# The first mixer takes x times the norm's weights, its tiles are multiplied by the root as they leave PSUM, and the opening is reordered

## The reference

```python
hn = rmsnorm(h, norm_mix_g)            # h * rsqrt(mean(h*h) + eps) * g, mean over the 2048 features
proj = hn @ w_in + b_in
(q, k, v, o_pre, i_pre, f_pre, cb, cc, ch, gm_pre, gc_pre) = jnp.split(proj, offs, axis=-1)
hm = mlstm_chunkwise(q, k, v, i_pre, f_pre)      # 4 heads, q and k 128 wide, v 256 wide
hm = hm * rsqrt(mean(hm*hm) + EPS) * mlstm_head_g * sigmoid(o_pre)
y_m = hm @ w_branch_m
y_c = (cb * causal_dwconv(cc * ch, conv_w)) @ w_branch_c
merged = sigmoid(gm_pre) * y_m + sigmoid(gc_pre) * y_c
h = h + merged @ w_out
```

## Time and profile before

| | us |
|---|---|
| median of 3 runs (lowest, highest) | 2176.17 (2174.1, 2178.84) |
| the profiled execution's own time | 2177.88 |
| its span, first to last instruction | 2175.8 |
| TensorE busy, matmuls | 2110.0 (97%) |
| VectorE busy | 1313.0 (60%) |
| ScalarE busy | 1159.3 (53%) |
| GpSimd busy | 280.0 (13%) |

### The profile page before, as it was taken

How to read it: one execution, slowest core, us unless ns; L and a number is a source line. 1 busy time by engine, 2 the same in 40 slices (tenths; PEclk the granted TensorE clock), 3 DMA queues, 4 the chain that set the end, 5 groups by cost and what they waited for, 6 DMA issues and landing times.

```text
span 2175.8 us, 46737 instructions
## 1 busy us (share of the span) xinstructions
PE 2110.0 (97%) x17596; PEld 2071.1 (95%) x17596; DVE 1313.0 (60%) x1662; ACT 1159.3 (53%) x1558; POOL 280.0 (13%) x325
## 2 busy tenths in 40 slices
PE   5999999999999999999999999999999979999996
PEld 5999999999999999999999999999998969999996
DVE  5656655444457777777775555575665565766644
ACT  5444545555445656565655444645555445566643
POOL 2000000000110111111111101111001123111112
PEclk8999999999999999999999999999999989999998
DMA  4455455555555555555555655455444533444443
GB/s 153 170 179 190 172 175 197 185 200 193 185 188 206 193 193 193 193 193 193 193 193 195 224 218 209 173 180 194 174 158 171 192 135 136 175 154 156 171 174 116
DMA packets 54927, 393.83 MB, mean 181 GB/s; under 512 B 6097, under 2 KB 6225, under 8 KB 7522
## 3 DMA queue, kind: packets, MB, share of 16 engines
q1 hardware_dynamic: 54432, 392.19, 50.4%
q10 hardware_dynamic: 450, 1.02, 0.1%
HBM read 391.09 MB, written 2.10 MB: 181 GB/s over the span
## 4 chain that ended last, share of the span: by engine, by line
PE 83%; issue 11%; DVE 2%; POOL 2%; ACT 1%; DMA 0%; DVEq 0%; POOLq 0%; ACTq 0%; SPq 0%
PE acc L574 24%; PE acc L575 24%; PE acc L576 24%; PE tok L619 2%; PE tok L621 2%; PE tok L620 2%; POOL sumsq_g L1983 1%; PE att L647 1%; POOL n_lo L1992 0%; PE att L878 0%; PE att L879 0%; POOL x L2005 0%; DVE w_lo L1385 0%; DVE rstd L1393 0%; PE att L821 0%
## 5 line engine op out<-in xcount | busy, mean ns | idle before, releaser
L1385 DVE TENSOR_TENSOR w_lo<-raw,w_hi 128x1024 fp32r<-128x1024 f32 x740 | 904.1, 1235 | 710.9 <-ACT w_hi L955 708.5
L955 ACT ACTIVATE w_hi<-raw 128x1024 fp32r<-128x1024 f32 x740 | 768.3, 1056 | 552.1 <-PE acc L576 295.1
L574 PE MATMUL acc<-n_hi,w_hi 128*128 128x256 f32 x3488 | 974.2, 279 | 23.9 <-POOL n_lo L1992 20.3
L575 PE MATMUL acc<-n_lo,w_hi 128*128 128x256 f32 x3488 | 968.7, 278 | 0.0
L576 PE MATMUL acc<-n_hi,w_lo 128*128 128x256 f32 x3488 | 968.6, 278 | 0.0
L574 PEld LDWEIGHTS acc<-n_hi,w_hi 128*128 128x128 f32 x3488 | 658.9, 189 | 27.3 <-issue 20.5
L575 PEld LDWEIGHTS acc<-n_lo,w_hi 128*128 128x128 f32 x3488 | 659.7, 189 | 0.5
L576 PEld LDWEIGHTS acc<-n_hi,w_lo 128*128 128x128 f32 x3488 | 658.9, 189 | 0.0
L574 PE MATMUL acc<-f_hi,w_hi 128*128 128x256 f32 x688 | 189.9, 276 | 0.0
L575 PE MATMUL acc<-f_lo,w_hi 128*128 128x256 f32 x688 | 189.9, 276 | 0.0
L576 PE MATMUL acc<-f_hi,w_lo 128*128 128x256 f32 x688 | 189.9, 276 | 0.0
(11 more groups left out here) (324 smaller groups left out, 2959.7 us busy)
## 6 DMA issues: line engine op xcount, KB each, us to landing
raw<-stream_in SPq DMA_DIRECT2D x370, 1024.0 KB, 4.8
x<-x_in SPq DMA_DIRECT2D x4, 512.0 KB, 7.6
out<-x SPq DMA_DIRECT2D x4, 512.0 KB, 2.7
v_bias<-v_bias_in ACTq DMA_DIRECT2D x1, 512.0 KB, 8.9
par<-params_in ACTq DMA_DIRECT2D x1, 287.0 KB, 5.5
pos_i<-positions_in ACTq DMA_DIRECT2D x1, 128.0 KB, 6.8
gk<-gk_in ACTq DMA_DIRECT2D x1, 68.0 KB
```

The lines of the kernel that those rows point to most:

```text
L574: nc.tensor.matmul(out, w_hi[:, s, wc], hi[:, k, :], start=first, stop=False)
L575: nc.tensor.matmul(out, w_hi[:, s, wc], lo[:, k, :], start=False, stop=False)
L955: nc.scalar.activation(w_hi[:, s, :], raw[:, s, :], ACT.Copy).then_inc(hi_ready, 1)
L1385: nc.vector.tensor_tensor(w_lo[:, s, :], raw[:, s, :], w_hi[:, s, :].bitcast(fp32), ALU.subtract).then_inc(lo_ready, 1)
```

## The change

The first layer's matmuls take x * g, without the root. ScalarE makes `n_hi` from x and the weights (`first_high`) and VectorE `n_lo` (`first_low`), tile by tile as x arrives; GpSimd's part and the normed tiles go. The squares come later: ScalarE makes them after the first six units (`first_squares`), VectorE adds them to one tile (`squares_step`), and TensorE adds that over partitions with two fp32r matmuls in the middle of head 0's values.

Loads: SP loads x group 0, the gates' first unit, x group 1, the queries' first unit, x groups 2 and 3, and then the second units of both. Positions and value bias move from ScalarE's queue to SP's, behind units 4 and 5. TensorE does the gates' first half, the queries' first half, and then both second halves side by side, tile by tile. The gates go to `att[0]` instead of an accumulator.

Every tile of the heads and of the merge's gates is taken from PSUM by VectorE with a multiplication by `rstd` (`scaled_out`). ScalarE's bias and sigmoid steps then work in place in SBUF, after the split of the same j instead of before it. Values (tokens on partitions) are multiplied by a column `rcol` that TensorE makes from `rstd` with two small matmuls.

Head 0 is written out ahead of the loop, which runs over heads 1 to 3. In it the order is: queries, keys, values (with the sum of squares after two units), output gates 0 and 1, decays and scores, the first `cc` tile, the weighted values, two tiles, the second `cc` tile, the head's sum, and the last two tiles. The gates' logarithms, the row work and the angles (in five parts) lie between its units on ScalarE and VectorE; the sine and cosine come after it. Heads 1 to 3 keep their order. The buffers of the angles move onto those of the norm.

```diff
         def _(sp):
-            for g in range(KT // 4):
-                sp.dma_start(x[:, 4 * g:4 * g + 4, :], x_in[:, 4 * g:4 * g + 4, :])\
-                    .then_inc(x_loaded[g], 16)
-            for c in range(2):
-                sp.dma_start(raw[:, 2 * c:2 * c + 2, :], ...
+            load_x(0)
+            sp.dma_start(raw[:, 0, :], stream_in[0, :, 0:UNIT]).then_inc(first_loaded, 16)
+            load_x(1)
+            sp.dma_start(raw[:, 1, :], stream_in[1, :, 0:UNIT]).then_inc(raw_ready[0], 16)
+            load_x(2)
+            load_x(3)
+            sp.dma_start(raw[:, 2:4, :], stream_in[0:2, :, UNIT:2 * UNIT]...).then_inc(raw_ready[1], 16)
+            sp.wait_ge(lo_ready, 2)
+            sp.dma_start(raw[:, 0:2, :], stream_in[2]...).then_inc(raw_ready[0], 16)
+            sp.dma_start(v_bias..., v_bias_in.to_broadcast(...)).then_inc(bias_loaded, 16)
+            sp.dma_start(pos_i..., positions_in.to_broadcast([P, T])).then_inc(pos_loaded, 16)
+            sp.wait_ge(lo_ready, 4)
+            sp.dma_start(raw[:, 2:4, :], stream_in[3]...).then_inc(raw_ready[1], 16)
...
# TensorE
-            norm_sum_all("mix")
-            feature_tile("gates", None, 0, 0, 0, n_hi, n_lo, wait_act=0)
+            def first_half(o, u, half):
+                pe.wait_ge(lo_ready, u + 1)
+                for c in range(8):
+                    k = 8 * half + c
+                    pe.wait_ge(xlo_ready, k + 1)
+                    last = tile(o, u, c, n_hi, n_lo, k, k == 0, k == KT - 1)
+                last.then_inc(unit_done, 1)
+            first_half(o_gates, 0, 0)
+            first_half(o_query, 1, 0)
+            pe.wait_ge(lo_ready, 4)
+            for k in range(8, KT):
+                pe.wait_ge(xlo_ready, k + 1)
+                last = tile(o_gates, 2, k - 8, n_hi, n_lo, k, False, k == KT - 1)
...
+                last = tile(o_query, 3, k - 8, n_hi, n_lo, k, False, k == KT - 1)
...
+            feature_tile("mix", 0, 2, 0, 0, n_hi, n_lo)
+            token_tiles("mix", 0, 4, 4, 4, M_DV, n_hi, n_lo, between=mix_sum)
+            pe.wait_ge(rstd_ready, NORM["mix"] + 1)
+            for t in range(2):
+                last = nc.tensor.matmul(att[3][:, T + t:T + t + 1], rstd[0:1, ...], ones[0:1, 0:1], ...)
+            last.then_inc(mcol_made, 1)
+            feature_tile("mix", 0, 8, 1, 1, n_hi, n_lo)
+            feature_tile("mix", 0, 10, 0, 1, n_hi, n_lo)
+            decays(0)
+            decay_scores(0)
+            feature_tile("mix", 0, 12, 1, 2, n_hi, n_lo)
+            weighted_values(0)
...
+            with pe.Fori(1, M_HEADS) as i:
...
# ScalarE
+            def first_high(k):
+                if k % 4 == 0:
+                    act.wait_ge(x_loaded[k // 4], 16)
+                nc.scalar.activation(n_hi[:, k, :], x[:, k, :], ACT.Identity,
+                                     scale=pcols("g_mix")[:, k:k + 1]).then_inc(xhi_ready, 1)
+            for k in range(KT):
+                if k == 2:
+                    act.wait_ge(first_loaded, 16)
+                    nc.scalar.activation(w_hi[:, 0, :], raw[:, 0, :], ACT.Copy).then_inc(hi_ready, 1)
+                if k == 6:
+                    act.wait_ge(raw_ready[0], 16)
+                    nc.scalar.activation(w_hi[:, 1, :], raw[:, 1, :], ACT.Copy).then_inc(hi_ready, 1)
+                if k == 12:
+                    high(2, 2, 0)
+                    high(3, 3, 0)
+                first_high(k)
             split("gates", None, 0)
             split("gates", None, 1)
+            for g in range(KT // 4):
+                first_squares(g)
...
                     split("mix", i, j)
+                    if first and j == 0:
+                        act.wait_ge(msum_added, 5)
+                        nc.scalar.activation(msum_hi[:, :], squares_all[:, 0, :], ACT.Copy)...
+                    if first and j == 3:
+                        norm_std("mix")
+                    if first and j == 6:
+                        gate_rows()
+                    if first and j == 7:
+                        gate_logs_of_rows()
+                    if j == (7 if first else 1):
+                        taken(act, 1, "mix", i, 0)
+                        nc.scalar.activation(qT[:, :], qT[:, :], ACT.Identity, ...).then_inc(qk_ready, 1)
...
+                    if j in (9, 11):
+                        n = (j - 9) // 2
+                        taken(act, 1 - n, "mix", i, 1)
+                        nc.scalar.activation(sig_o[:, n, :], sig_o[:, n, :], ACT.Sigmoid, ...)
# VectorE
+            def first_low(k):
+                dve.wait_ge(xhi_ready, k + 1)
+                nc.vector.scalar_tensor_tensor(
+                    out=n_lo[:, k, :], in0=x[:, k, :], scalar=pcols("g_mix")[:, k:k + 1],
+                    in1=n_hi[:, k, :].bitcast(fp32), op0=ALU.mult, op1=ALU.subtract).then_inc(xlo_ready, 1)
+            for k in range(KT):
+                if k == 2:
+                    rest(0, 0)
+                if k == 6:
+                    rest(1, 1)
+                if k == 12:
+                    rest(2, 2)
+                    rest(3, 3)
+                first_low(k)
+            def scaled_out(name, i, j, b, to):
+                unit_is_done(name, i, j)
+                nc.vector.tensor_tensor(to, acc[b][:, 0:T], rstd[:, :], ALU.mult).then_inc(acc_taken[b], 1)
...
+                    if first and j == 1:
+                        squares_step(2, 4, 4, 12)
+                        squares_step(3, 4, 2, 2)
+                        squares_step(4, 4, 1, 1)
...
+                    if first and j == 4:
+                        norm_rstd("mix")
+                        gate_rows()
+                    if j == (4 if first else 1):
+                        scaled_out("mix", i, 1, 1, qT[:, :])
+                    if j == (5 if first else 3):
+                        scaled_out("mix", i, 3, 0, kT[:, :])
...
+                    if first and j == 8:
+                        gate_sums_of_logs()
+                    if j in (9, 11):
+                        scaled_out("mix", i, j, 1 - n, sig_o[:, n, :])
...
+                    if first and j in (9, 10, 11, 16, 18):
+                        angles((9, 10, 11, 16, 18).index(j))
                     split("mix", i, j)
# GpSimd
-            norm_low("mix")
```

More of the change, by code:

```diff
@@ L1035, in _, with gate_logs_of_rows, mix @@
+            def gate_logs_of_rows():
+                chain.link(nc.scalar.activation(f_exp[32:64, :], f_abs[32:64, :], ACT.Exp, scale=-1.0))
+                nc.scalar.activation(f_log[32:64, :], f_exp[32:64, :], ACT.Ln, bias=1.0).then_inc(row_log, 1)
+            def mix(i):
+                first = isinstance(i, int)
+                late = LATE if first else 0
+                for j in range(24):
+                    if j == (12 if first else 5):
                         act.wait_ge(h_ready, FREE + i)
@@ L1099, in _ @@
                     split("merge", i, j)
+                    if jj in (1, 3):
+                        n = jj // 2
+                        taken(act, 1 - n, "merge", i, 2 * m)
+                        gate = (sig_m, sig_c)[n]
+                        nc.scalar.activation(gate[:, :], gate[:, :], ACT.Sigmoid,
+                                             bias=par_merge[:, i, 2 * m + n:2 * m + n + 1])\
+                            .then_inc(branch_ready, 1)
             def last_splits(name, per):
@@ L1479, in _ @@
+                        values(i, 0)
+                        if first:
+                            values(i, 1)
+                    if j == (12 if first else 8):
                         dve.wait_ge(scores_ready, i + 1)
@@ L1548, in _ @@
                                                     ALU.mult).then_inc(hm_ready, 1)
+                    if first and j in (9, 10, 11, 16, 18):
+                        angles((9, 10, 11, 16, 18).index(j))
                     split("mix", i, j)
-                chain.done(M_HEADS)
+            mix(0)
+            with dve.Fori(1, M_HEADS) as i:
+                chain.loop(i - 1, 13)
+                mix(i)
+                chain.done(M_HEADS - 1)
             with dve.Fori(0, KT // 2) as i:
@@ L1554, in _ @@
                     m, jj = divmod(j, 6)
+                    if jj in (1, 3):
+                        n = jj // 2
+                        dve.wait_ge(acc_taken[1 - n], FREE + count(2 - n, "merge", i, 2 * m))
+                        scaled_out("merge", i, j, 1 - n, (sig_m, sig_c)[n][:, :])
                     if jj in (4, 5):
```

355 lines of the change are left out of this document (208 added, 147 removed).

## The result

The kernel before ran in 2174.10 to 2178.84 us beside the first four runs of the changed kernel (median 2177.01). These took 2159.16, 2165.42, 2204.54 and 2205.24 us, at a granted clock of 0.985 to 0.988. So the runs of the changed kernel fall into two groups some 42 us apart, five short and six long; the ratio to before, 0.9931 with an interval of 0.9903 to 0.9958, is that of the short runs among the first four. The middle one of all eleven is 2197.85 us, so as it stands the changed kernel loses time about as often as it gains it. Forecast were 2154 us and a range of 2149 to 2162; four of the five short runs lie in it. The long ones are the rival to which I gave 0.05, at 2196. In 42 runs of before, none was above 2181.58.

What follows compares the result with a forecast made beforehand. TensorE hardly waits from 44 us on, so the gain lies before. 24.7 - 0.65 - 3.1 + 0.6 + 1.6 - 0.8 = 22.3 us off 2177.9 gives 2155.5; the median, 1.7 lower, is 2154, range 2149 to 2162.

Steps and rivals of the forecast that it cites:

- The opening: Start to the end of gates and queries: first matmul at 9.3, done at 23.4, 24.7 us gained.
- the second halves wait for 17.8: Opening: second halves of gates and queries start at 17.8, then take 5.6 us.
- Head 0's chain: Head 0, from root through ScalarE and VectorE to weights and masks at 62.7: TensorE, there at 59.6, waits 3.1 us.
- the case for which I had named 1.8 us: Head 0: if the sigmoid's table load runs ahead of its wait, TensorE waits 1.8 us before the weighted values.
- The 5.5 us: Head 0's chain: with a 1.38 us drain more per table load, the wait is 5.5 us longer, the time 2159.5.
- The rows wait: Head 0: the old wait for VectorE's row work before the decays goes, 0.6 us gained.
- the low clock: Head 0, behind the rows wait: 0.50 grant goes, 1.6 us gained; the new wait may bring it back, half counted, 0.8.
- the added matmuls: Head 0 on TensorE: two-matmul sum of squares, 0.25 us, and the root's column, some 0.4; together 0.65 us lost.
- Heads 1 to 3: Ten evictions a head move to VectorE, 4.2 us more in some 70; claimed to cost nothing.
- The merge: 32 evictions move to VectorE, 13.4 us more; accumulator wanted again 5.4 us later, so claimed to cost nothing.
- The rival by the pace: One short eviction wait in the merge restarts TensorE at the slower pace, 4.4 ns per matmul, 42 us: 2196; chance 0.05.
- Evictions have 5 us of room: Heads and merge: argument against the slower pace, with the up projection keeping the faster pace under the same work.

Runs made afterwards that it cites:

- e6_in_turn: Changed kernel, merge's convolution gate evicted ahead of the low half; opening's second halves one after the other, x tiles 12 to 15 before units 2 and 3; median 2159.55 us.
- e7_x_first: Changed kernel, merge's convolution gate evicted ahead of the low half; all four x groups loaded before any unit; median 2165.21 us.
- e5a_sig_late: Changed kernel, merge's convolution gate evicted ahead of the low half; head 0's output gate sigmoids put behind the decays' exponentials; median 2157.51 us, ratio 0.9920.
- e8_twice: Changed kernel, merge's convolution gate evicted ahead of the low half; evictions issued twice in heads 1 to 3; three runs 2157.41 to 2162.39 us, one 2199.37.
- e5_no_wait: e5a_sig_late with the five parts of head 0's rotary angles also moved later; median 2155.04 us, ratio 0.9906.
- e9_all: e5_no_wait and e6_in_turn combined, with ScalarE's gate rows and logarithms made at j = 5 in place of 6 and 7; median 2157.06 us, ratio 0.9907.
- e2_pace: Changed kernel, merge's convolution gate evicted ahead of the low half; the sum over the head's squares repeated before the merge; median 2198.76 us, ratio 1.0106.
- e11_values_late: e9_all plus one fp32 matmul before the latent attention's output product, and head 0's values leaving PSUM at j = 9 in place of 7; 2152.95 us, ratio 0.9897.

## Why the prediction was right, and where not

- **The number: right for the short runs, and that the first four held two of them was chance.** Of eleven runs five were short. Their gain is some 18.4 us by the profile where 22.3 were forecast; the points below say where the difference arose.
- **The opening: right, 1.2 us too good.** First matmul 9.56 for 9.3, first halves done at 17.0 for 16.8, gates and queries at 24.6 for 23.4. The step "the second halves wait for 17.8" left out that the loop alternates between units 2 and 3 and so needs both low halves; e6_in_turn gives this back. Matmuls at half rate (0.21 us apart) stood only from 9.56 to 13.75, 20 of 48, as taken. The column of the granted clock reads 1.00 there (9.5 to 13.8), as it does in the window of the old sums; the half rate is read from the distance of the matmuls alone. e7_x_first shows what the loads' order is worth by itself: 2.6 us. The rest was not taken apart by a run; in the profile it is the wait for normed tiles and the fp32 sums that are gone.
- **Head 0's chain: the wait right, the way to it partly luck.** The wait is 2.87 us for 3.1, but two misses of about 2 us each cancelled. The logarithm ended at 47.77 and not 45.4, since ScalarE waited 0.87 and 1.50 us for units' loads that I had not counted, and TensorE came 1.8 us later than I had it, to 61.4. The sigmoid's table load ran ahead of its wait (it stands at 50.62, the sigmoid at 54.75), the case for which I had named 1.8 us. At the end VectorE waits 0.70 us for ScalarE's last decay; e5a_sig_late shows that without this its own queue holds the weighted values nearly as long.
- **Loads without a drain.** From the exponential's table load to the end of the logarithm it is again 3.44 us (44.33 to 47.77). The 5.5 us that follow from the Trainium skill's page ScalarE: Activation LUTs (What ACT_TABLE_LOAD costs) did not show.
- **Small terms.** The rows wait went, but only 0.4 us with it: the decays start 0.42 us after the matmul ahead of them, and 0.85 before. Of the low clock I counted half; it came in full (0.51 from 65 to 68, below). From the weighted values to the sum of squares it is 20.06 us here and 18.41 in e6_in_turn, without the low clock and also at the faster pace: 1.65 us where I had 0.8. The sum had no term for pace, and needed none here: head 0's sum of squares turned it to the slower one up to head 1's decays, but before ran at the slower one ahead of that sum, so that from the queries' end to head 1's decays there are 286 matmuls at the slower pace now and 267 before, 0.1 us. So 1.2 (opening), 0.9 (low clock) and 0.2 (rows wait) make 2.3 of the 2.7 us by which 22.3 became 19.6; the rest is in terms of a tenth each, as the added matmuls (0.77 for 0.65).
- **Heads 1 to 3: right.** No wait there, and e8_twice doubles the evictions without an effect in these heads.
- **The merge: wrong, and this is the one step that failed outright.** "An accumulator is wanted again after the next tile, 5.4 us later; the eviction stands in front of one low half" holds for the heads and the up projection. In the merge the convolution's gate is followed by one unit of 24 matmuls, 2.7 us, before its accumulator is wanted, and in this order the low half stands in front of the eviction and can wait for ScalarE's table load. Its direct cost is 1.15 us, the way from 19.6 to 18.5.
- **The rival by the pace: its mechanism, place and price were right, its chance was not.** The wait is a short one, for an eviction in the merge, and the slower pace behind it costs 40.6 us (42 forecast). The rival had 0.05, and six of eleven runs were long. "Evictions have 5 us of room" was my argument against it, and that is the number that was not worked out where it mattered: in the merge it is 2.7 us. The range holds four of the five short runs and none of the long ones.

## What to carry to other kernels

When an eviction moves to another engine, work out its room at each place where the accumulator is reused, in that engine's queue order, not only at the place where it is usual. A dense TensorE stretch can inherit one of two paces from what stands ahead of it, so a wait of a microsecond must be priced with all matmuls up to the next break (here 9,170, 40.6 us), and a kernel with such a wait needs several runs before its time is believed. Moving one late step forward on one queue often only moves the wait to the next queue (e5_no_wait, e9_all): follow the chain through both.

## What the runs showed of the hardware

- Dense matmuls of one form run 0.1134 or 0.1178 us apart at a granted clock of 1.00, over stretches of up to 1080 us. The head's sum of squares, a single fp32 matmul of 256 columns, turned the faster pace to the slower in all five cases in which it met it (head 0 in four of the profiles here, and e2_pace). The slower it turned to the faster in heads 1 to 3 of all twelve profiles of the changed kernel and its variants, but in head 0 only in five of eight.
- After the wait of about a microsecond in the merge, to judge by the times, the stretch went on at the faster pace in five runs and at the slower in six. Behind the two shorter breaks of e8_twice's profile (0.15 and 0.23 us) it was the faster both times. What sets it there was not found.
- A pace can be chosen, where nothing waits in between: one fp32 matmul, which took 0.24 us (2043.32 to 2043.56), made a product of 768 matmuls 3.3 us shorter.
- The low clock came behind the wait at the weighted values in some executions (0.51 from 65 to 68 behind 2.87 us, the last line; also behind 2.04 us in e7_x_first) and not in others (1.00 behind 2.58 us in e6_in_turn and 1.76 in e5a_sig_late), so the length of the wait does not decide it here. In e11_values_late it came without any wait that the profile shows. The Trainium skill's page TensorE: Matmul & The Clock Gate (HAM oscillation) has waits between bursts bring it back; the first cases agree, e6_in_turn, e5a_sig_late and e11_values_late do not follow it.

```profile
65.00:68.00 3.00, 3.00 (x13) 2.64 (x12) 1.78 (x3) 0.75 (x2) 0.00 (x0) 0.51 0.71 254
```
